# The norms' factors computed on columns with tokens on the partitions, in a two-block transformer kernel

## The chip, the cores and the metric

The kernel runs on one core of one Trainium2 chip. The metric is the device time of one execution in microseconds (us), the median of three. Five engines work on their own queues of instructions, each in order: TensorE (PE in the profile; its weight loads are PEld), VectorE (DVE), ScalarE (ACT), GpSimd (POOL) and SyncE (SP), which issues the weights' transfers. They meet at semaphores.

## The reference

Everything is fp32, one batch, T = 256 tokens, width D = 2048. Two blocks follow each other; the norms are what matters here.

```python
def rms_norm(x, g):
    y = x * lax.rsqrt(jnp.mean(x * x, axis=-1, keepdims=True) + 1e-6)
    return y * g

def first_block(x, mem, ...):            # two layers
    mem_n = rms_norm(mem, mem_norm_g)    # 256 memory tokens, read by 4 heads per layer
    for l in range(2):
        h = rms_norm(x, norm_g[l])
        z = h @ w_in[l]                  # q, k, v and gates of three kinds of attention
        ...                              # neighbourhood, dilated and memory attention
        x = x + y @ w_out[l]
    return rms_norm(x, final_g)

def layer_norm(x, g, b, eps=1e-5):
    mu = x.mean(-1, keepdims=True)
    var = jnp.square(x - mu).mean(-1, keepdims=True)
    return (x - mu) * lax.rsqrt(var + eps) * g + b

def second_block(x, positions, ...):     # ALPHA = sqrt(2)
    for layer in range(2):
        x = layer_norm(ALPHA * x + mixers[layer](x), *ln1[layer])
        x = layer_norm(ALPHA * x + conv_ffn(x, *ffns[layer]), *ln2[layer])
    return x

def mla_rwkv_mixer(x, ...):              # mixers[0]
    c_q, c_kv, k_pe = split_cols(mla_p, (448, 128, 64))
    q = rms_norm_2(c_q, q_norm) @ w_uq   # a norm over 448 latent ranks
    kv = rms_norm_2(c_kv, kv_norm) @ w_ukv   # and one over 128
    ...
```

Each norm needs, for every token, one factor (the reciprocal root of the mean square or the variance), and a layer norm also the shift, minus the mean times the factor.

## The kernel before

The activations lie with features on the 128 partitions and tokens along the free axis: x is 16 tiles of 128x256. The weights (579.8 MB read in all) stream through four raw buffers of 128x1024. ACT rounds each to a high half (`hi`, L2688), DVE subtracts to get the low half (`lo`, L3026), and TensorE does three matmuls for each 128x128 block, high by high, high by low and low by high (`col`, L2185 to L2187, "main matmuls" below). One buffer of weights is 24 of them.

The order of work is written by a Python planner. `do(name, ...)` appends a step to a plan, and each engine's program replays the plan in that order, so every engine has a fixed queue. Side work (norms, attention heads, memory) is written as generators; `pump()` advances each of them by one `yield` after every buffer of weights. A `yield` between two steps therefore sets 24 main matmuls between them on TensorE. `load` keeps the high halves four buffers ahead (AHEAD = 4), and five pairs of halves exist. PSUM is eight banks, handed out by `bank()` and given back with the event that frees them.

Factors are made at ten places. Seven are a `Norm` (class at L717): two for the first block's layers (kind "pre"), the first block's last one, four layer norms. Two generators call `rms_job` (L711): `mem_norm` in `first()` for the memory, and `rank_norms` for q_norm (four tiles) and kv_norm (one tile), so three jobs.

In all of them the squares are summed over the partitions by a matmul with a 128x128 matrix of ones stationary and 256 tokens streamed (`norm_sums`, L2265 and L2266; `rms_sq`, L2247 for each tile). The result is a 128x256 block in a bank in which every partition holds the same sums. The arithmetic is then done on the whole 128x256 block: DVE makes the variance (L3080 to L3087, L3089, L3034), ACT the root (L2705, L2701), DVE the reciprocal (L3094, L3036) and for a layer norm the product (L3097). The result R is a row of factors on all partitions, ready for products with tokens on the free axis: `rms_scale` L3041, `norm_ln` L3140 and L3142, `norm_rms` L3148, `lead_scale` L3134, `lead_fix`, `q_scale` L3184, `gate_evict` L3199 and L3201.

The first block's v has tokens on the partitions, so its two norms also need the factor as a column: `norm_cols` (L2272) takes R through TensorE, two matmuls of one streamed column, into a second bank, and DVE copies it out (L3101) for `v_scale` on ACT.

The memory's attention touches the change too: scores (L2291 to L2293), row maxima on DVE (L3235), exponentials on ACT (L2782, with a table load), normalising on DVE (L3244 to L3247), turning by TensorE (L2302), copies by ACT and DVE (L2773, L3178) and the product with v (L2313 to L2315).

## Time and profile before

| what | us |
|---|---|
| median of 3 runs | 3438.81 (3436.49 to 3444.06) |
| profiled execution | 3437.72 |
| its span in the trace | 3435.9 |
| TensorE busy (weight loads) | 3349.4, 97% (3267.1, 95%) |
| DVE busy | 2304.6, 67% |
| ACT busy | 1629.0, 47% |
| GpSimd busy | 60.2, 2% |
| mean granted TensorE clock | 0.989 of full speed |

The span runs from the first to the last instruction; the profiled execution's own time is 1.8 us longer. Busy times are of single engines and overlap. In the timeline rows, the first column is the start in us from the start of the span, the second the length; in brackets stands the idle time of the engine before the instruction and what ended it. A matmul's length includes its passage through the array, so the distance between two starts (0.11 to 0.12 us for a main matmul), not the length (0.28), is what it costs. An fp32 matmul can be two rows (x2).

### The profile page before, as it was taken

What the parts mean: (1) busy time and instruction counts of PE and PEld (TensorE: products, weight loads), DVE (VectorE), ACT (ScalarE), POOL (GpSimd) and SP (SyncE); (2) the same over time, 40 slices, a digit from 0 to 9 for tenths busy, and PEclk for the clock granted to TensorE, in tenths of its full rate; (3) what the DMA queues carried; (4) which work ended last, traced back from release to release, by engine and by line L of the source; (5) the groups of instructions that cost most, each with busy time, mean ns of one, the idle gap of its engine ahead of it and who ended that gap; (6) DMA issues with size and microseconds to landing.
All of it is one profiled execution on the core that took longest, in us unless ns stands there. A gap on an engine that the chain in (4) does not pass through costs nothing.

```text
span 3435.9 us, 67619 instructions
## 1 busy us (share of the span) xinstructions
PE 3349.4 (97%) x29402; PEld 3267.1 (95%) x29402; DVE 2304.6 (67%) x3765; ACT 1629.0 (47%) x2389; POOL 60.2 (2%) x78
## 2 busy tenths in 40 slices
PE   8999999999999899999999999999999999999997
PEld 8999999999999889999999999998999999999997
DVE  6677656667776787796666555686656966666455
ACT  6444544444555434464444444563443644444443
POOL 0000000000000000000000000001000000000000
PEclk9999999999999999999999999999998999999998
DMA  7555555555554223356555665543434565555563
GB/s 247 176 172 181 180 178 180 188 181 181 175 192 141 89 87 105 111 184 198 192 193 193 196 194 189 177 154 103 157 129 138 170 206 193 193 193 191 188 202 126
DMA packets 162489, 586.29 MB, mean 171 GB/s; under 512 B 18128, under 2 KB 18128, under 8 KB 161936
## 3 DMA queue, kind: packets, MB, share of 16 engines
q1 hardware_dynamic: 160560, 574.01, 51.5%
q0 software_dynamic: 1632, 7.96, 0.7%
q8 instruction: 230, 3.77, 0.5%
q14 instruction: 67, 0.55, 0.1%
HBM read 579.80 MB, written 2.10 MB: 169 GB/s over the span
## 4 chain that ended last, share of the span: by engine, by line
PE 53%; DVE 8%; ACT 1%; issue 0%; POOL 0%; ACTq 0%; DVEq 0%; POOLq 0%
PE bank L2185 16%; PE bank L2187 16%; PE bank L2186 16%; DVE pairs L3026 2%; PE bank L2422 1%; PE bank L2435 1%; DVE xs L3142 1%; DVE xs L3140 1%; PE bank L2200 0%; PE bank L2201 0%; PE bank L2202 0%; DVE xr L3030 0%; DVE right L3513 0%; DVE xr L3110 0%; ACT pairs L2688 0%
## 5 line engine op out<-in xcount | busy, mean ns | idle before, releaser
L2185 PE MATMUL bank<-xr,pairs 128*128 128x256 f32 (+1 forms) x5888 | 1656.9, 281 | 31.0 <-DVE pairs L3026 25.6
L2186 PE MATMUL bank<-xr,pairs 128*128 128x256 f32 (+1 forms) x5888 | 1640.0, 279 | 0.0
L2187 PE MATMUL bank<-xr,pairs 128*128 128x256 f32 (+1 forms) x5888 | 1639.6, 278 | 0.0
L2688 ACT ACTIVATE pairs<-raw 128x1024 fp32r<-128x1024 f32 x1106 | 1144.2, 1042 | 945.4 <-PE bank L2187 716.8
L3026 DVE TENSOR_TENSOR pairs<-raw,pairs 128x1024 fp32r<-128x1024 f32 x1106 | 1311.2, 1202 | 298.2 <-ACT pairs L2688 292.7
L2185 PEld LDWEIGHTS bank<-xr,pairs 128*128 128x128 f32 x5888 | 1114.4, 189 | 43.5 <-DVE pairs L3026 28.3
L2186 PEld LDWEIGHTS bank<-xr,pairs 128*128 128x128 f32 x5888 | 1112.6, 189 | 0.9
L2187 PEld LDWEIGHTS bank<-xr,pairs 128*128 128x128 f32 x5888 | 1113.4, 189 | 0.0
L2185 PE MATMUL bank<-parts,pairs 128*128 128x256 f32 x1792 | 496.2, 277 | 0.4 <-DVE parts L3030 0.4
L2187 PE MATMUL bank<-parts,pairs 128*128 128x256 f32 x1792 | 495.3, 276 | 0.0
L2186 PE MATMUL bank<-parts,pairs 128*128 128x256 f32 x1792 | 495.3, 276 | 0.0
L2185 PEld LDWEIGHTS bank<-parts,pairs 128*128 128x128 f32 x1792 | 336.6, 188 | 0.7 <-DVE parts L3030 0.6
L2186 PEld LDWEIGHTS bank<-parts,pairs 128*128 128x128 f32 x1792 | 336.5, 188 | 0.1
L2187 PEld LDWEIGHTS bank<-parts,pairs 128*128 128x128 f32 x1792 | 336.4, 188 | 0.0
L3487 DVE TENSOR_SCALAR arena<-bank,vec 128x256 f32<-128x256 f32 x88 | 47.8, 543 | 204.2 <-PE bank L2187 204.1
L3154 DVE SCALAR_TENSOR_TENSOR xs<-xs,bank 128x512 f32<-128x512 f32 x64 | 43.5, 686 | 158.9 <-PE bank L2187 158.9
L2713 ACT ACTIVATE nbuf<-xs 128x512 f32<-128x512 f32 x56 | 35.4, 632 | 121.7 <-DVE xs L3056 89.6
L2237 PE MATMUL bank<-pairs,xr 128*128 128x512 f32 x192 | 76.9, 401 | 0.0
L2185 PE MATMUL bank<-yr,pairs 128*128 128x256 f32 x256 | 72.6, 284 | 3.4 <-DVE yr L3030 3.4
L2239 PE MATMUL bank<-pairs,xr 128*128 128x512 f32 x192 | 75.7, 394 | 0.0
L2238 PE MATMUL bank<-pairs,xr 128*128 128x512 f32 x192 | 75.2, 392 | 0.0
L2186 PE MATMUL bank<-yr,pairs 128*128 128x256 f32 x256 | 72.1, 282 | 0.0
(621 smaller groups left out, 3231.6 us busy)
## 6 DMA issues: line engine op xcount, KB each, us to landing
raw<-in_w_in SPq DMA_DIRECT2D x176, 512.0 KB, 4.9
raw<-in_gate SPq DMA_DIRECT2D x176, 512.0 KB, 5.7
raw<-in_val SPq DMA_DIRECT2D x176, 512.0 KB, 4.2
raw<-in_down SPq DMA_DIRECT2D x160, 512.0 KB, 4.4
raw<-in_l_w_in SPq DMA_DIRECT2D x144, 512.0 KB, 4.0
raw<-in_w_out SPq DMA_DIRECT2D x64, 512.0 KB, 4.5
raw<-in_l_w_out SPq DMA_DIRECT2D x64, 512.0 KB, 3.8
raw<-in_v_in SPq DMA_DIRECT2D x48, 512.0 KB, 3.9
```

The costliest lines, as they stand in the source:

```text
L2185: mm(o, wh[:, q, :], rh[:, k, :], start=begin and q == 0, stop=False)
L2186: mm(o, wh[:, q, :], rl[:, k, :], start=False, stop=False)
L2187: last = mm(o, wl[:, q, :], rh[:, k, :], start=False, stop=end and q == c - 1)
L2237: mm(o, lh[:, k, ms], wh[:, q, :], start=k == 0, stop=False)
L2238: mm(o, ll[:, k, ms], wh[:, q, :], start=False, stop=False)
L2239: last = mm(o, lh[:, k, ms], wl[:, q, :], start=False, stop=k == KT - 1)
L2422: last = mm(p4[b, g, :], j.XT[b, g, 64:128], j.X[b, g, :], start=True, stop=True)
L2688: e.activation(pair_of(n)[0], v3(raw_of(n), widths[n] // slices[n]), ACT.Copy).then_inc(*hi_made(n))
L2713: e.activation(N.sq, x[:, t:t + 2, :], ACT.Square).then_inc(*act("norm_sq", N.id, t))
L3026: e.tensor_tensor(lo_, v3(raw_of(n), widths[n] // slices[n]), hi_.bitcast(F32), SUB).then_inc(*lo_made(n))
L3154: e.scalar_tensor_tensor(out=x[:, t:t + 2, :], in0=x[:, t:t + 2, :], scalar=alpha, in1=v3(bk.view, 2), op0=MUL, op1=ADD).then_inc(*vec("x_ ...
L3487: e.tensor_scalar(b, p2[:, 0, :], VC(f"cw2_{l}", t), VC(f"cb_{l}", t), MUL, ADD).then_inc(*vec("conv2", j.id))
```

## The change

The sums get the squares as the stationary operand and one column of ones as the streamed one. The result is one column for each 128 tokens with the tokens on the partitions, so two columns for all. Variance, root, reciprocal and product run on 128x2 blocks in the factor buffer (`nfac`, or two columns for each rms job; `nbuf` is 12 columns wider). The pause (`yield`) between variance and reciprocal goes, one comes after the reciprocal, and behind it stand `norm_rows` or `rms_rows`: TensorE transposes of the column, broadcast along the free axis, give the same row block in a bank as before, and ACT copies it to where R was. Users of the row wait for ACT's copy ("nR", "R" of ACT); `v_scale` takes the columns as they are, and `norm_cols` with its bank is gone. The sums' bank is kept until the copy.

```diff
-    nbuf = sb("nbuf", 6 * T + 12)
+    nbuf = sb("nbuf", 6 * T + 24)
...
+    nfac = nbuf[:, 6 * T + 12:6 * T + 18]
...
@@ class Norm, rows
             yield from self.sums()
-            yield
-            self.bk2 = yield from bank()
-            do("norm_cols", self)
-            banks.put(self.bk2, (vec, "cols", self.id))
@@ class Norm, sums
             do("norm_sums", self)
             yield
             do("norm_var", self)
-            banks.put(self.bk, (vec, "nvar", self.id))
-            yield
             do("norm_R", self)
+            yield
+            do("norm_rows", self)
+            banks.put(self.bk, (act, "nR", self.id))
@@ mem_norm
             do("rms_R", r)
-            banks.put(r.bk, (vec, "var", r.id))
+            yield
+            do("rms_rows", r)
+            banks.put(r.bk, (act, "R", r.id))
@@ rank_norms
             for r in rs:
                 do("rms_R", r)
-                banks.put(r.bk, (vec, "var", r.id))
+            yield
+            for r in rs:
+                do("rms_rows", r)
+                banks.put(r.bk, (act, "R", r.id))
@@ TensorE's program
-            mm(r.bk.view[:, 0:T], ones[rows], r.sq[t].view[rows], start=t == 0, stop=t == r.n - 1).then_inc(*pe("rms", r.id, t))
+            for m in range(2):
+                last = mm(r.bk.view[:, m:m + 1], r.sq[t].view[rows, m * 128:(m + 1) * 128], ones[rows, 0:1],
+                          start=t == 0 and m == 0, stop=t == r.n - 1)
+            last.then_inc(*pe("rms", r.id, t))
+
+        def rms_rows(r):
+            w.wait_ge(*vec["rcol", r.id])
+            for m in range(2):
+                last = e.transpose(r.bk.view[:, T + m * 128:T + (m + 1) * 128], r.f[:, m:m + 1].broadcast_to([128, 128]), ident)
+            last.then_inc(*pe("rrows", r.id))
...
-            if N.kind == "ln":
-                mm(ps[:, 0:T], ones, N.a1, start=True, stop=True)
-            mm(ps[:, T:2 * T], ones, N.a2, start=True, stop=True).then_inc(*pe("norm_sums", N.id))
-
-        def norm_cols(N):
-            w.on(N.bk2.after)
-            w.wait_ge(*vec["nR", N.id])
-            for m in range(2):
-                last = mm(N.bk2.view[:, m:m + 1], N.a2[:, m * 128:(m + 1) * 128], ident[:, 0:1], start=True, stop=True)
-            last.then_inc(*pe("cols", N.id))
+            for i, src in enumerate((N.a1, N.a2)):
+                if i or N.kind == "ln":
+                    for m in range(2):
+                        c = 2 * i + m
+                        last = mm(ps[:, c:c + 1], src[:, m * 128:(m + 1) * 128], ones[:, 0:1], start=True, stop=True)
+            last.then_inc(*pe("norm_sums", N.id))
+
+        def norm_rows(N):
+            w.wait_ge(*vec["ncol", N.id])
+            for c in range(0 if N.kind == "ln" else 2, 4):
+                last = e.transpose(N.bk.view[:, c * 128:(c + 1) * 128], N.f[:, c:c + 1].broadcast_to([128, 128]), ident)
+            last.then_inc(*pe("nrows", N.id))
@@ ACT's program
         def rms_R(r):
             w.wait_ge(*vec["var", r.id])
-            e.activation(r.R, r.R, ACT.Sqrt).then_inc(*act("std", r.id))
+            e.activation(r.f, r.f, ACT.Sqrt).then_inc(*act("std", r.id))
+
+        def rms_rows(r):
+            w.wait_ge(*pe["rrows", r.id])
+            e.activation(r.R, r.bk.view[:, T:2 * T], ACT.Copy).then_inc(*act("R", r.id))
...
+        def norm_rows(N):
+            w.wait_ge(*pe["nrows", N.id])
+            if N.kind == "ln":
+                e.activation(nbuf[:, 4 * T:6 * T], N.bk.view, ACT.Copy).then_inc(*act("nR", N.id))
+            else:
+                e.activation(N.a2, N.bk.view[:, T:2 * T], ACT.Copy).then_inc(*act("nR", N.id))
...
-            w.wait_ge(*vec["nR", j.norm.id])
+            w.wait_ge(*act["nR", j.norm.id])
@@ DVE's program
-            e.tensor_scalar(r.R, r.bk.view[:, 0:T], 1.0 / r.width, 1e-6, MUL, ADD).then_inc(*vec("var", r.id))
+            e.tensor_scalar(r.f, r.bk.view[:, 0:2], 1.0 / r.width, 1e-6, MUL, ADD).then_inc(*vec("var", r.id))
             w.wait_ge(*act["std", r.id])
-            e.reciprocal(r.R, r.R).then_inc(*vec("R", r.id))
+            e.reciprocal(r.f, r.f).then_inc(*vec("rcol", r.id))
...
-            ps, R, nm = N.bk.view, N.a2, N.a1
+            ps, nm, R, m2 = N.bk.view, N.f[:, 0:2], N.f[:, 2:4], N.f[:, 4:6]
...
-                e.tensor_scalar(nm, ps[:, 0:T], -1.0 / D, None, MUL).then_inc(*vec("mean", N.id))
+                e.tensor_scalar(nm, ps[:, 0:2], -1.0 / D, None, MUL).then_inc(*vec("mean", N.id))
...
-            R, nm = N.a2, N.a1
+            nm, R = N.f[:, 0:2], N.f[:, 2:4]
             w.wait_ge(*act["nstd", N.id])
-            e.reciprocal(R, R).then_inc(*vec("nR" if N.kind != "ln" else "nR0", N.id))
+            e.reciprocal(R, R).then_inc(*vec("ncol" if N.kind != "ln" else "nR0", N.id))
```

How the queues change is shown at two places. The lines are numbered by each kernel's own text: before's L2688, L2692, L2760, L2773 and L2782 are L2707, L2711, L2790, L2803 and L2812 now, L3026, L3140 and L3142 are L3056, L3165 and L3167.

ACT's queue at the memory's norm, before: the root of the memory's factors (L2701), then a high half, then the table and the exponentials of the memory attention.

```order
L2701 ACT_TABLE_LOAD
L2701 ACTIVATE arena<-arena 128x256
L2688 ACTIVATE pairs<-raw 128x8x128
L2782 ACT_TABLE_LOAD
L2782 ACTIVATE arena<-arena 128x256 x4
L2688 ACTIVATE pairs<-raw 128x8x128
L2692 ACTIVATE parts<-hs 128x256
L2760 ACTIVATE arena<-bank 128x256
L2773 ACTIVATE heads<-bank 128x512 x2
L2692 ACTIVATE parts<-hs 128x256
```

The same place now:

```order
L2720 ACT_TABLE_LOAD
L2720 ACTIVATE nbuf<-nbuf 128x2
L2707 ACTIVATE pairs<-raw 128x8x128
L2724 ACTIVATE arena<-bank 128x256
L2812 ACT_TABLE_LOAD
L2812 ACTIVATE arena<-arena 128x256 x4
L2707 ACTIVATE pairs<-raw 128x8x128
L2790 ACTIVATE arena<-bank 128x256
L2711 ACTIVATE parts<-hs 128x256
L2803 ACTIVATE heads<-bank 128x512 x2
```

The copy of the rows, L2724, now stands between the high half and the exponentials' table load. On TensorE its two transposes (L2263) stand 48 main matmuls behind the scores and 24 ahead of the turning of the probabilities, which before stood 72 behind the scores.

DVE's queue at layer 0's first layer norm, before: the last sums of squares, two low halves, the variance, a low half, reciprocal and product, a low half, and the first pair of tiles scaled (L3140).

```order
L3074 TENSOR_TENSOR nbuf<-nbuf 128x256
L3026 TENSOR_TENSOR pairs<-raw,pairs 128x8x128 x2
L3080 TENSOR_SCALAR nbuf<-bank 128x256
L3082 TENSOR_TENSOR nbuf<-nbuf 128x256
L3084 SCALAR_TENSOR_TENSOR nbuf<-bank,nbuf 128x256
L3087 TENSOR_SCALAR nbuf<-nbuf 128x256
L3026 TENSOR_TENSOR pairs<-raw,pairs 128x8x128
L3094 RECIPROCAL nbuf<-nbuf 128x256
L3097 TENSOR_TENSOR nbuf<-nbuf 128x256
L3026 TENSOR_TENSOR pairs<-raw,pairs 128x8x128
L3140 TENSOR_TENSOR xs<-xs,nbuf 128x512
```

The same place now:

```order
L3104 TENSOR_TENSOR nbuf<-nbuf 128x256
L3056 TENSOR_TENSOR pairs<-raw,pairs 128x8x128 x2
L3110 TENSOR_SCALAR nbuf<-bank 128x2
L3112 TENSOR_TENSOR nbuf<-nbuf 128x2
L3114 SCALAR_TENSOR_TENSOR nbuf<-bank,nbuf 128x2
L3116 TENSOR_SCALAR nbuf<-nbuf 128x2
L3123 RECIPROCAL nbuf<-nbuf 128x2
L3126 TENSOR_TENSOR nbuf<-nbuf 128x2
L3056 TENSOR_TENSOR pairs<-raw,pairs 128x8x128 x2
L3165 TENSOR_TENSOR xs<-xs,nbuf 128x512
```

The reciprocal stands directly behind the variance, with both low halves behind it. On TensorE the sums stay where they were, and the four transposes (L2291) stand 48 main matmuls behind them, as they do at every `Norm` but the last, where they follow at once.

## Rows read from the trace of the kernel before

**Rows 1.** the page: count, busy us, mean ns, idle us before, releaser.

```profile
L2185 PE MATMUL bank<-xr,pairs 128*128 128x256 f32 (+1 forms) x5888 | 1656.9, 281 | 31.0 <-DVE pairs L3026 25.6
```

**Rows 2.** timeline of TensorE around the memory's norm: start, us, line, idle before.

```profile
86.64 0.28 PE L2293 MATMUL bank<-heads 128*128 128x256 f32 x1
...
94.53 0.28 PE L2185 MATMUL bank<-xr,pairs 128*128 128x256 f32 x1
...
95.24 1.04 PE L2302 MATMUL bank<-con,arena 128*128 128x128 f32 x8
...
98.26 0.36 PE L2313 MATMUL bank<-heads 128*128 128x256 f32 x1 [1.97 <-DVE heads L3178]
```

**Rows 3.** the same stretch on ACT.

```profile
86.68 1.28 ACT L2782 ACT_TABLE_LOAD   x1
...
89.87 0.19 ACT L2782 ACTIVATION_READ_ACCUMULATOR arena<-arena 128x1 f32 x1
...
96.22 1.08 ACT L2773 ACTIVATE heads<-bank 128x512 fp32r<-128x512 f32 x2
```

**Rows 4.** the same stretch on DVE.

```profile
85.35 1.75 DVE L3036 RECIPROCAL arena<-arena 128x256 f32<-128x256 f32 x1 [1.96 <-ACT arena L2701]
...
94.76 0.16 DVE L3244 RECIPROCAL arena<-arena 128x2 f32<-128x2 f32 x1
...
97.43 1.28 DVE L3178 TENSOR_TENSOR heads<-bank,heads 128x512 fp32r<-128x512 f32 x2
```

**Rows 5.** busy time by stretch, PEclk the granted clock.

```profile
96.00:100.00 4.00, 2.03 (x15) 1.82 (x14) 3.11 (x7) 2.67 (x5) 1.09 (x1) 0.90 0.30 114
...
100.00:104.00 4.00, 4.00 (x26) 4.00 (x26) 3.54 (x6) 1.56 (x4) 0.00 (x0) 0.67 0.21 46
```

**Rows 6.** groups of instructions, each shape apart: busy us, mean ns.

```profile
L3244 DVE RECIPROCAL arena<-arena 128x2 f32<-128x2 f32 x40 | 6.3, 157 | 2.6 <-ACT arena L2782 2.3
...
L2760 ACT ACTIVATE arena<-bank 128x256 f32<-128x256 f32 x32 | 12.3, 384 | 122.4 <-DVE bank L3199 122.4
...
L2804 ACT ACTIVATE right<-bank 128x512 f32<-128x512 f32 x10 | 6.0, 598 | 11.4 <-PE bank L2375 10.6 <-PE bank L2346 0.5
```

**Rows 7.** the latent ranks' norms, on DVE, then TensorE.

```profile
1039.29 0.38 DVE L3041 SCALAR_TENSOR_TENSOR arena<-arena,vec 128x256 f32<-128x256 f32 x1
...
1047.88 0.38 PE L2185 MATMUL bank<-xr,pairs 128*128 128x256 f32 x1 [1.80 <-DVE pairs L3026]
...
1053.03 0.58 PE L2385 MATMUL bank<-con,right 128*128 128x2 f32 x4 [0.54 <-ACT right L2832]
```

**Rows 8.** layer 0's first layer norm: sums, 5.7 us of L2185, first user.

```profile
1476.08 0.38 PE L2266 MATMUL bank<-nbuf,con 128*128 128x256 f32 x1
...
1476.50:1482.20 5.70, 4.53 (x16) 2.91 (x16) 1.00 0.71 220
...
1483.19 0.68 DVE L3140 TENSOR_TENSOR xs<-xs,nbuf 128x512 f32<-128x512 f32 x1
```

**Rows 9.** the same two ends at the second and third layer norm.

```profile
2200.73 0.38 PE L2266 MATMUL bank<-nbuf,con 128*128 128x256 f32 x1
...
2207.34 0.68 DVE L3140 TENSOR_TENSOR xs<-xs,nbuf 128x512 f32<-128x512 f32 x1
...
2699.54 0.38 PE L2266 MATMUL bank<-nbuf,con 128*128 128x256 f32 x1
...
2706.68 0.68 DVE L3140 TENSOR_TENSOR xs<-xs,nbuf 128x512 f32<-128x512 f32 x1
```

**Rows 10.** the last norm, on DVE.

```profile
3416.66 0.42 DVE L3080 TENSOR_SCALAR nbuf<-bank 128x256 f32<-128x256 f32 x1 [1.28 <-PE bank L2266]
...
3421.05 0.69 DVE L3140 TENSOR_TENSOR xs<-xs,nbuf 128x512 f32<-128x512 f32 x1
```

**Rows 11.** two stretches of main matmuls: length, TensorE busy (count), granted clock.

```profile
422.80:507.90 85.10, 85.10 (x725) 85.07 (x723) 48.95 (x63) 39.20 (x49) 0.00 (x0) 1.00 0.57 179
...
898.70:980.10 81.40, 80.99 (x715) 80.80 (x713) 52.43 (x71) 40.90 (x54) 1.09 (x2) 1.00 0.60 199
```

54 lines of the change are left out of this document (27 added, 27 removed).

## The prediction

> **What bounds the kernel now.** I read the page's busy times first. TensorE is the bound: its main matmuls wait for little, and nearly all of that for the low halves of weights from DVE: the first of the three lines has 5888 matmuls and 31.0 us of idle time before them, 25.6 of it for L3026 [rows 1]. So DVE's saved time counts only where TensorE waits for DVE, and ACT's only where DVE waits for ACT. A norm's factors matter by the time at which their first user can start, and by what stands behind them in a queue. Next I read the timeline of the three engines around each of the ten places where factors are made, with the order of before and after beside it. They fall into five: the memory's norm, the latent ranks' norms, three layer norms under streamed weights, the last norm, and the rest.
>
> **The change part by part.** All chains run now: sums on TensorE, factor arithmetic on DVE and ACT (two columns), then, about one or two pumps later, transposes on TensorE, and a copy from the bank by ACT. The long DVE operations go, but the user waits for the second TensorE visit, which stands at a fixed place among the main matmuls. Below I ask only when that visit can come.
>
> *The memory's norm.* The last score matmul starts at 86.64 [rows 2]. In the changed order 48 main matmuls follow, then the two transposes. Six main matmuls took 0.71 us (94.53 to 95.24), 0.118 each [rows 2], so the transposes start at 86.76 + 5.66 = 92.4. Eight transposes took 1.04 us, 0.13 each [rows 2]; two end at 92.7. ACT copies 128x256 from a bank in 0.38 us [rows 6], with a hand-off on either side: 93.1. Now the queue: before, ACT began the exponentials' table at 86.68 and ended the last exponential at 90.06 [rows 3]. Now the copy stands in ACT's queue directly ahead of that table, so the table is loaded from 93.1 to 94.4 (1.28 us) and the four exponentials, 2.1 us from 87.98 to 90.06, end at 96.5, 6.4 us later than before. DVE's normalising of the second pair of rows began at 94.76 [rows 4], well after its exponentials, so 4.7 us of the 6.4 are cover; what is left over is 96.5 - 94.76 = 1.7 us. Behind the exponentials ACT has one high half (1.05), then the gate's tanh (which waits for DVE's L3199), a 0.4 us rounding and the copies of the turned probabilities, which began at 96.22 [rows 3]. I get 97.5 after the high half, DVE's row work and L3199 done by 97.8, tanh to 98.2, rounding to 98.6: 2.4 us later. These copies, with DVE's L3178 at 97.43 [rows 4], release the matmul that began at 98.26 after 1.97 us of idle TensorE [rows 2]. TensorE has nothing else in between, so the idle time grows to 4.4: **+2.4 us**. The reciprocal of 1.75 us on DVE that goes [rows 4] gives nothing, as its user, the scaling, isn't on that path. Behind this stop the granted clock falls: 0.90 in the 4 us around it and 0.67 in the next 4 [rows 5], that is 0.4 + 1.3 = 1.7 us of TensorE work lost already. A stop twice as long may add between nothing and as much again; I take the middle, **+0.8**. The ends for this place: +0 (the cover is larger than I think) and +2.4 + 1.7 + 0.4 for queue effects = +4.5.
>
> *The latent ranks' norms.* The scaling began at 1039.29 on DVE, right behind the second reciprocal [rows 7]. The two 1.75 us reciprocals go, but the transposes stand 48 main matmuls behind the last squares, and then ACT copies twice; I get the rows at about 1041.0, 1.7 later. What was late before is another thing too: TensorE stood 1.80 us at 1047.88 for a low half that DVE made behind the scaling [rows 7]. Two low halves now come ahead of the scaling in time, since DVE is free sooner, and this stop should go or shrink. But the user at 1053.03 waits for the chain that starts with the scaling [rows 7], and there the idle time comes back: the chain keeps its end within some tenths, as ACT's and DVE's pauses between its links (0.5 each) are filled differently. **0**, with ends -1.8 (stop gone and nothing back) and +1.7 (the whole lateness).
>
> *The three layer norms whose factors are used under weights* (layer 0's first and second, layer 1's first). The sums' second matmul started at 1476.08 and takes 0.44, to 1476.5. 16 L2185, so 48 main matmuls, took 5.70 us [rows 8]: 1482.2. Four transposes at 0.13: 1482.7. The 512-wide copy 0.60 [rows 6] and two hand-offs: 1483.4, against the first user at 1483.19 [rows 8]: +0.2. At the second the same working from 2200.73 gives 2208.1 against 2207.34, +0.8; at the third from 2699.54 gives 2706.9 against 2706.68, +0.2 [rows 9]. DVE saves in each norm the difference of six long operations and six short ones of 0.16 us [rows 6], near 3 us, but all of them lie ahead of a wait for the rows, so DVE just idles. After these points DVE is the engine that is late until TensorE stands for it, so I count the lateness in full, **+1.2**. The transposes' own 0.5 us fall into those stops. Ends: 0 and 1.2 + 3 x 0.5 = 2.7.
>
> *The last norm.* Here nothing covers anything. Before: DVE 3416.66 to the first scaling at 3421.05, 4.39 us [rows 10]. Now: four operations of 0.16 with 0.05 between them 0.8, a short root 0.25 (bounded by 0.42, the wide one's duration), reciprocal and product 0.4, four transposes 0.5 (up to 1.0 if the clock is low there), copy and hand-offs 0.7: 2.7 to 3.2. **-1.3**, ends -1.7 and -0.9.
>
> *The rest.* The two norms ahead of the first block's layers and the one that ends it: two matmuls with one streamed column replace one with 256. I have no row for such a one alone; it lies between a 128-column transpose, 0.13, and the 0.44 of the wide one, and I take 0.22, which makes the sums equal. The column step (two matmuls, DVE's copy, one bank) goes twice, -0.9; six transposes come, +0.8. Memory squares: 16 tiles at the same price. Their rows come when the reciprocal's result did, give or take 0.3. **0**, ends -1 and +1. The factor buffer is 12 columns wider, which moves what lies behind it by some bytes; no duration in the trace hangs on that.
>
> The transposes' price is the place where the notes speak against the change. The trace's eight took 0.13 us each. The Trainium skill (TensorE: Matmul & The Clock Gate, Part 4: PE-mode transpose) gives about 275 ns for one inside a kernel and says that they don't count as busy time for the clock. By that figure the change's 28 transposes would take 4 us more than mine, of which the half in open places would show: the sum would be 2 us higher. The measured 0.13 decides; whether the clock takes them as idle no row here shows.
>
> **Sum**: +2.4 + 0.8 + 0 + 1.2 - 1.3 + 0 = +3.1. The profiled execution took 3437.7 us (span 3435.9 and 1.8 around it), which gives 3440.8. The median of the timed runs, 3438.8, lies 1.1 above the profiled one, so the median of the changed kernel would be 3440.8 to 3441.9; I say **3441.5**.
>
> **Rivals.** *A: the rows are not what comes last (faster).* If the wait that I see at 1482.7 is covered, DVE's saving of 2.7 to 3 us in each of three norms reaches TensorE, which waits mostly for DVE [rows 1]: -8.1. With the ranks' stop gone (-1.8), the end's -1.3 and only +1 at the memory's norm the time is 3437.7 - 10.2 = 3427.5. For it: the waits for L3026. Against it: the 48 matmuls [rows 8], which no faster engine shortens. *B: ACT's copy holds back high halves (slower).* Behind each copy in ACT's queue stand the high halves that were made before at some 3 us earlier; in the three layer norms a late half of 2.7 us means a late low half and a stop of TensorE. It decides if fewer than two finished pairs lie ready when the copy waits. Price 3 x 2.7 = 8.1 instead of the 1.2 counted: 3440.8 + 6.9 = 3447.7. For: three of the long waits for L3026 follow layer norms. Against: none begins within 15 us of the copies. *C: the pitch of the main matmuls flips.* They run at one of two pitches at full clock: 725 in 85.1 us, 0.1174 each, and 715 in 81.4, 0.1138 [rows 11]. I see flips behind groups of small matmuls, and the change edits such groups. One stretch of 720 at the other pitch is 2.6 us, of either sign; two are 5.2. That gives 3436 to 3447. *D: nothing of it reaches the end*, because the memory's stall was already as long as its cover allows and the clock recovers: 3438.
>
> **How the numbers follow.** Forecast 0.38, A 0.12, B 0.14, C 0.20, D 0.16. A measurement of this kernel can tell about 0.2%, 6.9 us, from no change: faster is under 3431.9, slower above 3445.7. Faster: A, and a small part of C, 0.13. Slower: B, a quarter of C and a rest of the forecast, 0.20. Same: 0.67. The unknown costs' ends lie below the sum by 3.2 (memory), 1.8 (ranks), 1.2, 1 and 0.4, and above it by 1.3, 1.7, 1.5, 1 and 0.4; as not all fall on one side at once, the forecast's own range is 3436 to 3446; with C's second stretch and part of A and B it becomes 3433 to 3450.
>
> **What would show it.** ACT idle for some 6 us before its 256-wide copy of the memory's factors, and TensorE idle for over 4 us before the first probability matmul: right. If that stop is still near 2 us, the memory's term is wrong. DVE idle for 3 to 4 us before the first scaling of each layer norm: right; if it is busy there, A. TensorE waits for L3026 within 10 us behind a layer norm's copy: B. The wait at 1047.88 smaller and the one at 1053 larger: the ranks' term. The first scaling of the last norm 3.1 us behind the end of its sums: the last term. The same number of main matmuls in a longer or shorter stretch without any idle time: C.

## The result and the profile after

The changed kernel took 3444.24 us (median of 20 runs, 3439.35 to 3449.95) against 3439.02 us for the kernel before (20 runs, 3434.24 to 3445.67). The ratio is 1.0015, 95% interval 1.0009 to 1.0021: slower by 0.15%, 5.2 us, with 3 to 7 us in the interval. That is inside the 0.2% that the prediction called no change, and inside its range; it said 2.7 us for the medians. For the profiled execution it said 3.1 us; that execution has a span of 3444.0 us, 8.1 above the one before.

The page of the changed kernel, as answer to [rows 1] (L2193 is what L2185 was, L3056 what L3026 was):

```profile
span 3444.0 us, 67794 instructions
...
PE 3352.3 (97%) x29486; PEld 3271.7 (95%) x29486; DVE 2286.1 (66%) x3763; ACT 1630.8 (47%) x2399; POOL 59.9 (2%) x78
...
L2193 PE MATMUL bank<-xr,pairs 128*128 128x256 f32 (+1 forms) x5888 | 1654.1, 281 | 32.1 <-DVE pairs L3056 24.8
```

The waits of the main matmuls on low halves are what they were, 24.8 against 25.6 us. DVE's busy time is 18.5 us lower, and nothing of it shows in the span.

Because every main matmul (23,808 in all) is in both traces in the same order, the start of each can be subtracted from the start of the same one in another trace. This table holds, for stretches of the kernel (named by the times of the kernel before), how much longer the stretch took than in the first trace of the kernel before, in us. It is worked out from the start times of both traces, to about 0.1 us; "end" is from the last main matmul to the end of the span.

| kernel | 12-70 | 70-130 memory | 130-540 | 540-975 | 975-1022 | 1022-1100 ranks | 1150-1240 | 1475-1600 LN | 2195-2330 LN | 2330-2700 | 2700-2760 LN | end |
|---|---|---|---|---|---|---|---|---|---|---|---|---|
| before, second trace | +1.2 | +0.2 | 0.0 | +2.9 | +0.2 | 0.0 | 0.0 | -0.3 | +0.1 | -3.2 | +0.2 | +0.9 |
| changed | +0.8 | +2.5 | -0.8 | +0.5 | +1.8 | +1.1 | +2.8 | +0.6 | +1.0 | -4.1 | +1.1 | -0.4 |
| changed, second trace | +0.4 | +2.1 | -1.6 | +3.4 | +0.7 | +3.0 | +3.1 | +0.2 | +0.9 | -1.6 | +0.3 | -1.0 |

The two traces of one kernel show what a single one can tell: many stretches agree within 0.4 us, but 12 to 70, 540 to 975, 2330 to 2700, the end and, in the changed kernel, 130 to 540, 975 to 1022, the third layer norm's and the ranks' stretch move by 0.6 to 3 us by themselves. What repeats is +2.3 at the memory's norm, +0.2 to +1.1 at each layer norm and 3 us between 1150 and 1240; the end is about 1.2 shorter in the mean (-0.7 against +0.45).

**The memory's norm.** ACT in the changed kernel, as answer to [rows 3]: start, length, in brackets the idle time before.

```profile
94.20 0.38 ACT L2724 ACTIVATE arena<-bank 128x256 f32<-128x256 f32 x1 [5.79 <-PE bank L2263]
94.61 1.28 ACT L2812 ACT_TABLE_LOAD   x1
...
97.79 0.18 ACT L2812 ACTIVATION_READ_ACCUMULATOR arena<-arena 128x1 f32 x1
...
101.64 1.06 ACT L2803 ACTIVATE heads<-bank 128x512 fp32r<-128x512 f32 x2
```

TensorE in the same stretch, as answer to [rows 2] (L2263 the new transposes, L2321 the turning of probabilities, L2332 the product with v):

```profile
88.02 0.28 PE L2312 MATMUL bank<-heads 128*128 128x256 f32 x1
...
93.79 0.38 PE L2263 MATMUL bank<-con,nbuf 128*128 128x128 f32 x2
...
97.90 0.66 PE L2321 MATMUL bank<-con,arena 128*128 128x128 f32 x4 [1.00 <-DVE arena L3272]
99.73 0.66 PE L2321 MATMUL bank<-con,arena 128*128 128x128 f32 x4 [1.17 <-DVE arena L3272]
103.08 0.55 PE L2332 MATMUL bank<-heads 128*128 128x256 f32 x1 [2.70 <-DVE heads L3203]
```

The last score matmul is at 88.02, 1.38 later than before by what lies ahead. From it the transposes are 5.77 us away, the copy comes after 5.79 us of idle ACT, and the last exponential ends at 97.97 instead of 90.06: 7.9 later, 6.5 net of the 1.38. The single stop of 1.97 us has become three, of 1.00, 1.17 and 2.70, together 4.87. The probability product starts 4.82 us later, 3.4 of it the change's. Behind it a part comes back, at the end 0.16 us in every 4 by a faster pitch of the main matmuls; at 130 us 2.5 are left. The stops differ between two traces of one kernel too: the second trace of the kernel before has 2.82 us where the first has 1.97, the second of the changed kernel 1.00, 0.33 and 3.18. In the mean of two traces each that is 4.7 against 2.4 us, 2.3 more.

**The layer norms.** DVE at layer 0's first layer norm, as answer to [rows 8]:

```profile
1487.25 0.15 DVE L3110 TENSOR_SCALAR nbuf<-bank 128x2 f32<-128x2 f32 x1
...
1488.47 0.16 DVE L3126 TENSOR_TENSOR nbuf<-nbuf 128x2 f32<-128x2 f32 x1
...
1493.56 0.69 DVE L3165 TENSOR_TENSOR xs<-xs,nbuf 128x512 f32<-128x512 f32 x1 [2.65 <-ACT nbuf L2733]
```

The six short operations take 1.4 us from 1487.25 to 1488.63 with the root among them; two low halves follow, and then DVE idles 2.65 us for ACT's copy. Net of what lies ahead (10.0 us by then) the first scaling starts 0.37 later than before. The stops of TensorE behind it are as long as they were: the first is 2.13 and 1.81 us in the two traces of the changed kernel, 2.13 and 1.79 in those of the kernel before.

**The last norm.** As answer to [rows 10], DVE:

```profile
3425.93 0.16 DVE L3110 TENSOR_SCALAR nbuf<-bank 128x2 f32<-128x2 f32 x1 [2.02 <-PE bank L2285]
...
3429.15 0.69 DVE L3165 TENSOR_TENSOR xs<-xs,nbuf 128x512 f32<-128x512 f32 x1 [1.84 <-ACT nbuf L2733]
```

From the first operation to the first scaling it is 3.22 us, before 4.39.

**The ranks' norms.** TensorE's waits in the whole span, as answer to the stops of [rows 7]:

```profile
PE bank L2404 <- ACT right L2862: 5.3, 3, 3.9
```

The longest, 3.9 us, is the user that stood 0.54 us before; the stop of 1.80 for a low half is gone. The user itself is not late: it starts at 1057.91, 4.9 us behind the 1053.03 of the kernel before, and TensorE was 5.5 us late already at 1022. Yet the stretch lost 1.1 and 3.0 us, and nothing in the second trace of the kernel before. What lies elsewhere is time at half clock: both traces of the kernel before have 3.41 us of it ahead of the user (from 1048.1 in the first), the changed kernel behind it (from 1058.4), and its second trace 3.41 us more from 1032.5, where it falls back by 1.6.

### The profile page after: what moved, and what is told of

Read it like the earlier page. It is cut to its first block, busy times and chain, and to the rows that moved or that the text cites. A ratio compares the mean times of both kernels' runs of the same rounds, so it can differ in the third digit from the quotient of the medians.

```text
span 3444.0 us, 67794 instructions
## 1 busy us (share of the span) xinstructions
PE 3352.3 (97%) x29486; PEld 3271.7 (95%) x29486; DVE 2286.1 (66%) x3763; ACT 1630.8 (47%) x2399; POOL 59.9 (2%) x78
## 4 chain that ended last, share of the span: by engine, by line
PE 89%; DVE 7%; ACT 2%; issue 1%; DMA 1%; POOL 0%; ACTq 0%; SPq 0%; DVEq 0%; POOLq 0%
PE bank L2193 25%; PE bank L2195 24%; PE bank L2194 24%; DVE pairs L3056 2%; PE bank L2245 2%; PE bank L2247 2%; PE bank L2246 2%; PE bank L2441 1%; PE bank L2454 1%; DVE xs L3167 1%; ACT pairs L2707 1%; DVE xr L3060 1%; DVE xs L3165 1%; DMA raw<-in_w_in 0%; PE bank L2208 0%
## 5 line engine op out<-in xcount | busy, mean ns | idle before, releaser
L2193 PE MATMUL bank<-xr,pairs 128*128 128x256 f32 (+1 forms) x5888 | 1654.1, 281 | 32.1 <-DVE pairs L3056 24.8
L2707 ACT ACTIVATE pairs<-raw 128x1024 fp32r<-128x1024 f32 x1106 | 1144.0, 1042 | 932.9 <-PE bank L2195 726.9
L3056 DVE TENSOR_TENSOR pairs<-raw,pairs 128x1024 fp32r<-128x1024 f32 x1106 | 1310.4, 1202 | 296.0 <-ACT pairs L2707 290.4
L2193 PEld LDWEIGHTS bank<-xr,pairs 128*128 128x128 f32 x5888 | 1111.5, 189 | 43.3 <-DVE pairs L3056 27.2
L2193 PE MATMUL bank<-parts,pairs 128*128 128x256 f32 x1792 | 495.9, 277 | 0.4 <-DVE parts L3060 0.4
L2193 PEld LDWEIGHTS bank<-parts,pairs 128*128 128x128 f32 x1792 | 336.4, 188 | 0.6 <-DVE parts L3060 0.6
L2193 PE MATMUL bank<-yr,pairs 128*128 128x256 f32 x256 | 72.2, 282 | 4.1 <-DVE yr L3060 4.1
```

What stands on the lines that cost most here:

```text
L2193: mm(o, wh[:, q, :], rh[:, k, :], start=begin and q == 0, stop=False)
L2707: e.activation(pair_of(n)[0], v3(raw_of(n), widths[n] // slices[n]), ACT.Copy).then_inc(*hi_made(n))
L3056: e.tensor_tensor(lo_, v3(raw_of(n), widths[n] // slices[n]), hi_.bitcast(F32), SUB).then_inc(*lo_made(n))
```

## The experiments

All medians stand beside runs of the kernel before on the same chip; with 11 or 12 runs they carry an interval of about 0.9 thousandths, 3 us, to each side (ln_rows24, 6 runs, 1.4 thousandths). So the place of an effect is read from the stretches, the medians only confirm large ones. The stretches of all kernels, against the first trace of before:

| kernel | ratio (95% interval) | 70-130 memory | 975-1022 | 1022-1100 ranks | 1150-1240 | 1475-1600 LN | 2195-2330 LN | 2700-2760 LN | end |
|---|---|---|---|---|---|---|---|---|---|
| changed | 1.0015 (1.0009-1.0021) | +2.5, +2.1 | +1.8, +0.7 | +1.1, +3.0 | +2.8, +3.1 | +0.6, +0.2 | +1.0, +0.9 | +1.1, +0.3 | -0.4, -1.0 |
| mem_undone | 1.0010 (1.0000-1.0020) | +0.3 | +1.8 | +2.7 | +2.8 | +0.4 | +0.9 | +0.3 | -1.1 |
| mem_copy_later | 1.0017 (1.0008-1.0026) | -0.2 | +0.7 | +3.0 | +2.9 | +0.9 | +0.9 | +0.1 | -0.5 |
| ranks_undone | 1.0018 (1.0008-1.0027) | +1.9 | +1.8 | +1.8 | +2.8 | +0.2 | +0.9 | +0.6 | -0.5 |
| ln_undone | 1.0015 (1.0006-1.0024) | +2.7 | +1.8 | +2.7 | +3.0 | 0.0 | +0.1 | +0.8 | +0.8 |
| rms_undone | one run | +3.4 | 0.0 | +1.4 | +2.8 | +0.4 | +1.0 | +1.1 | -0.4 |
| rms_rows24 | 0.9998 (0.9989-1.0007) | -0.8 | +1.8 | +0.3 | +1.7 | +0.4 | +0.9 | +0.6 | -0.8 |
| norm_rows_early | 1.0009 (1.0000-1.0018) | +3.7 | +1.8 | +2.0 | +0.4 | -0.2 | +0.2 | -0.7 | -1.3 |
| all_pace | 1.0002 (0.9994-1.0011) | +0.4 | +1.8 | +4.9 | +2.9 | -0.4 | +0.2 | -0.2 | -0.7 |
| all_rows_early | 0.9995 (0.9986-1.0004) | -0.8 | +0.6 | +2.3 | +0.4 | -0.2 | +0.2 | 0.0 | -1.2 |
| ln_rows24 | 1.0048 (1.0035-1.0062) | +2.5 | +0.7 | +3.1 | +3.1 | +1.1 | +3.7 | +2.9 | -1.3 |

Five edits leave the memory's norm as the changed kernel has it (ranks_undone, ln_undone, rms_undone, norm_rows_early, ln_rows24). With the changed kernel's own two traces the memory's stretch is then +1.9 to +3.7. TensorE runs 3.41 us at half clock behind the stop in the four with +1.9 to +2.5, and 6.83 us in the three with +2.7 to +3.7.

### The memory's norm as before

```diff
+            if r.wide:   # the memory's job: PE, ACT, DVE steps of the kernel before
+                mm(r.bk.view[:, 0:T], ones[rows], r.sq[t].view[rows], start=t == 0, stop=t == r.n - 1).then_inc(*pe("rms", r.id, t))
+                return
...
             do("rms_R", r)
-            yield
-            do("rms_rows", r)
-            banks.put(r.bk, (act, "R", r.id))
+            banks.put(r.bk, (vec, "var", r.id))
```

> The changed kernel with the memory's norm alone as it was before (wide sums, wide root and reciprocal, no transposes, no copy). Theory (ACT's copy of the rows holds back the exponentials): ACT's 5.8 us of idle time before the copy and TensorE's longer stop before the first probability matmul go; that stop is near 2.0 us again instead of 2.7 behind two of about 1, the main matmuls behind it start about 2.8 us earlier against the changed kernel, and the median is 2 to 4 us lower. Rival (small matmuls and the pitch of the main ones make the difference, not this wait): the stop shrinks but the median moves by less than 1 us.

Measured: +0.3 instead of +2.5 and +2.1 in the memory's stretch, with one stop of 2.80 us in place of the three (not the 2.0 that was expected, but the 2.82 of the second trace of before); the ratio goes from 1.0015 to 1.0010, which is in the expected direction but not told apart by the interval. So 2 us belong to this place.

### ACT's copy behind the exponentials

The transposes stay where they are; only the step that holds ACT's copy is planned one pump later.

```diff
-            do("rms_rows", r)
-            banks.put(r.bk, (act, "R", r.id))
-            for t in range(KT):
-                yield
-                yield
+            do("rms_turn", r)      # TensorE's two transposes
+            yield
+            do("rms_copy", r)      # ACT's copy
+            banks.put(r.bk, (act, "R", r.id))
+            for t in range(KT):
+                if t:
+                    yield
+                yield
```

> The changed kernel with one instruction moved: ACT's copy of the memory's rows stands behind the four exponentials and the next high half instead of ahead of them; TensorE's and DVE's queues are the same. Theory (the copy in front of the exponentials is the whole cost at the memory's norm): the exponentials end near 91 us again, the stop before the first probability matmul is 2 to 3 us and those before the turning go, main matmuls behind it 2 to 2.8 us earlier than in the changed kernel. Rival (the transposes on TensorE, or DVE's later scaling, are the cost): TensorE reaches 130 us as late as in the changed kernel, within 0.7.

Measured, ACT (L2815 the exponentials, L2727 the copy), then TensorE (L2266 the transposes, L2335 the product with v):

```profile
86.99 1.28 ACT L2815 ACT_TABLE_LOAD   x1
...
90.18 0.18 ACT L2815 ACTIVATION_READ_ACCUMULATOR arena<-arena 128x1 f32 x1
...
93.14 0.38 ACT L2727 ACTIVATE arena<-bank 128x256 f32<-128x256 f32 x1 [1.82 <-PE bank L2266]
...
92.72 0.38 PE L2266 MATMUL bank<-con,nbuf 128*128 128x128 f32 x2
...
99.38 0.55 PE L2335 MATMUL bank<-heads 128*128 128x256 f32 x1 [2.67 <-DVE heads L3206]
```

The table load starts at 86.99, right behind the high half, the last exponential ends at 90.36, and the copy waits where nobody needs ACT. The three stops are one of 2.67 us again. The stretch 70 to 130 takes 0.2 us less than before and 2.3 to 2.7 less than in the changed kernel, with TensorE's and DVE's queues the same. The trace shows the mechanism by itself: neither the transposes nor the later rows cost more here than the 0.2 to 0.4 us by which a stretch scatters; the place of one 0.38 us copy in ACT's queue does. Its median (5.9 us over before, interval 2.7 to 8.9) does not show the gain: the stretch 540 to 975 took 3.4 us more in its trace, as in the second traces of both kernels, and that is the size of the interval that a median of 11 runs has. The proof rests on the stretches of the traces, not on the medians.

### The latent ranks' norms as before

The same edit for the other two jobs.

> The changed kernel with the latent ranks' norms alone as before. Theory: the stop of 3.9 us before the L2404 matmul goes back to 0.5 us and a stop of about 1.8 for a low half comes back 5 us ahead of it; net 0.5 to 1.5 us faster than the changed kernel. Rival (the ranks' norms cost what their later rows say, plus the stretches at half clock behind them at 1167, 1198 and 1283 us): 3 to 5 us faster.

Measured: +1.8 in the ranks' stretch, between the +1.1 and +3.0 of the changed kernel's own two traces; ratio 1.0018. The theory's 0.5 to 1.5 us do not come. The stop for a low half is back (1.71 us, with 0.39 ahead of it), but the user's goes from 3.9 to 2.14 and not to 0.5. The user starts at 1054.65, on time against its surroundings, but the 3.41 us at half clock still lie behind it (from 1055.5), and not ahead as in the kernel before. So no gain or loss of these norms is seen, and the stretch's 1 to 3 us go with the place of the half clock; no run moved that on purpose. The rival's 3 to 5 us are excluded for this stretch, and the 2.8 us between 1150 and 1240 stay.

### The layer norms as before

The same edit for the Norms of kind "ln".

> The changed kernel with the four layer norms as before (wide sums and arithmetic, no transposes); the other norms stay changed. Theory: the three layer norms under weights give back 1.2 us and TensorE's transposes there 0.3 each, and the last norm gets 0.4 us longer: 0.5 to 2 us faster than the changed kernel. Rival (the layer norms hold a large part of the 5 us): 3 us faster or more. Second rival (the layer norms were a gain): slower by 1 us or more.

Measured: 0.0 and +0.1 in the first two stretches where the changed kernel has +0.6, +0.2 and +1.0, +0.9; +0.8 in the third, which scatters. The end is 0.8 over the first trace of before, the second trace of before had 0.9. The ratio, 1.0015, is the changed kernel's. The theory's 0.5 to 2 us are not seen: its 0.4 for the last norm was too little (the end is 1.5 us longer than in the changed kernel's mean), which cancels the 1.3 us of the first two layer norms. None of this is clear of a median's interval of 3 us.

### Rows 24 main matmuls behind the sums, layer norms, pause removed

```diff
             do("norm_R", self)
-            yield
+            if self.kind != "ln":
+                yield
             do("norm_rows", self)
```

> The changed kernel, layer norms only: the pause between reciprocal and transposes removed, so that the transposes stand 24 instead of 48 main matmuls behind the sums. Theory (the rows are what comes last at the three layer norms, and DVE is what TensorE waits for afterwards): the first scaling of each starts 2.6 to 2.8 us earlier, TensorE's following stops for low halves shrink by as much, the median is 5 to 8 us lower than the changed kernel. Rival (those stops come from elsewhere, transfers or ACT): DVE's scaling starts earlier, but the stops stay and the median moves by less than 2 us.

Measured: 11 us slower than the changed kernel by the ratios, the opposite of both. The theory's first half held: DVE waited only 0.97 us for the copy, at 1490.29, and against its surroundings the first scaling starts 2.9 us earlier than in the changed kernel.

```profile
1490.29 0.69 DVE L3166 TENSOR_TENSOR xs<-xs,nbuf 128x512 f32<-128x512 f32 x1 [0.97 <-ACT nbuf L2734]
...
1517.62 0.38 PE L2194 MATMUL bank<-xr,pairs 128*128 128x256 f32 x1 [2.58 <-DVE pairs L3057]
```

But the removed pause lets the generators of side work run one buffer ahead, and the planner deals out other work to the following buffers. At 1517.62 TensorE stands 2.58 us for a low half that DVE made behind other work. In layer 1's mixer 5 us are lost in the stretch 2330 to 2560 against the changed kernel. The same 45 us of the clock hold 676 matmuls there and 582 here; as ln_rows24 is 3 to 7 us later at this point, the two windows do not hold the same work. The changed kernel,

```profile
2355.00:2400.00 45.00, 45.00 (x676) 42.68 (x675) 29.91 (x62) 18.40 (x31) 3.33 (x5) 1.00 0.37 118
```

and ln_rows24:

```profile
2355.00:2400.00 45.00, 44.00 (x582) 39.98 (x581) 26.92 (x55) 15.57 (x27) 3.34 (x5) 0.96 0.33 104
```

The edit had moved two things. That the moved side work is the cause is concluded from this; the next edit moves one thing only.

### The same rows, the pace of the side work kept

```diff
             do("norm_R", self)
-            yield
             do("norm_rows", self)
+            yield
             banks.put(self.bk, (act, "nR", self.id))
```

DVE's queue is now that of the changed kernel (but for one low half near 110 us, which stands one place earlier); only transposes and copy stand earlier, at every Norm.

> The changed kernel with the transposes of every Norm 24 instead of 48 main matmuls behind its sums, while the side work keeps its pace (the pause now stands behind the transposes), so that DVE's queue is the same and only the transposes and ACT's copy move. Theory (rows are what comes last at the three layer norms and DVE's lateness reaches TensorE; the slower ln_rows24 got slower because its side work moved by one buffer): the first scalings start 2.6 us earlier against their surroundings, DVE's idle time of 2.7 to 3.3 us before them goes, the stops for low halves behind them shrink by 1 to 2.6 us each, and the median is 3 to 7 us lower than the changed kernel's. Rival (earlier rows themselves do harm, as in ln_rows24): slower than the changed kernel by 5 us or more. Second rival (the stops are set by ACT's high halves or the transfers): within 1.5 us.

Measured: DVE no longer waits for the copy, but now it waits 1.92 us for a high half, ahead of the low half in front of the scaling. DVE, then ACT:

```profile
1486.60 1.22 DVE L3056 TENSOR_TENSOR pairs<-raw,pairs 128x1024 fp32r<-128x1024 f32 x1
1489.74 1.23 DVE L3056 TENSOR_TENSOR pairs<-raw,pairs 128x1024 fp32r<-128x1024 f32 x1 [1.92 <-ACT pairs L2707]
1490.88 0.69 DVE L3165 TENSOR_TENSOR xs<-xs,nbuf 128x512 f32<-128x512 f32 x1
...
1488.16 0.60 ACT L2733 ACTIVATE nbuf<-bank 128x512 f32<-128x512 f32 x1 [1.87 <-PE bank L2291]
1488.66 2.00 ACT L2707 ACTIVATE pairs<-raw 128x1024 fp32r<-128x1024 f32 x2
```

In ACT's queue that high half stands behind the copy, and the copy waits 1.87 us for the transposes: it is the memory's mechanism again, and that of the prediction's rival B. The idle time of DVE does not go, it shrinks from 2.65 to 1.92 us, by 0.7. The first scaling starts 0.8 us earlier against its surroundings, not 2.6.

The stop that was 2.13 us in the changed kernel's first trace (1.81 in its second) is 1.39:

```profile
1520.33 0.39 PE L2193 MATMUL bank<-xr,pairs 128*128 128x256 f32 x1 [2.13 <-DVE pairs L3056]
...
1524.32 0.39 PE L2193 MATMUL bank<-xr,pairs 128*128 128x256 f32 x1 [0.97 <-DVE pairs L3056]
```

```profile
1517.65 0.38 PE L2193 MATMUL bank<-xr,pairs 128*128 128x256 f32 x1 [1.39 <-DVE pairs L3056]
...
1521.65 0.39 PE L2193 MATMUL bank<-xr,pairs 128*128 128x256 f32 x1 [0.99 <-DVE pairs L3056]
```

The three stretches gain 0.6, 0.8 and 1.4 us on the changed kernel (mean of its traces), 2.7 together. The median ratio falls from 1.0015 to 1.0009, 2.1 us, inside the interval. The theory is right in kind and its 3 to 7 us were too many: it took DVE's whole idle time as won, and what TensorE got, 0.7 us of 2.13, is what was left of it once DVE waited for the high half. A copy placed behind that high half was not tried.

### The memory's and the ranks' rows 24 matmuls earlier; all together

rms_rows24 removes the pause ahead of `rms_rows` in both generators; all_pace moves all transposes ahead of their pauses; all_rows_early joins rms_rows24 and norm_rows_early.

> The changed kernel, memory's and latent ranks' norms only: the pause between reciprocal and transposes removed (24 instead of 48 main matmuls). Theory: ACT copies the memory's rows 2.8 us earlier, the exponentials end 2.8 us earlier, and since 4.7 us of delay were covered before, hardly any of the memory's 2.8 us are left; the ranks' user comes 2.5 us earlier too. Together 4 to 5.5 us faster than the changed kernel. Rival (the small instructions themselves and not their place cost the time): under 1.5 us.

> As norm_rows_early, and the memory's and the latent ranks' transposes 24 instead of 48 main matmuls behind the squares too, again with the pace kept. Theory: the two gains add, as they lie at different places: 7 to 12 us below the changed kernel, 2 to 6 below the kernel before. Rival (only the memory's place is worth anything): 4 to 6 us below the changed kernel, level with the kernel before.

> The version that the runs point to: the changed kernel with the memory's and the ranks' rows as in rms_rows24 and the Norms' rows as in norm_rows_early. Theory (effects at separate places add, the memory and ranks' 1.2 us better than the changed kernel's by the matmuls' times, the layer norms' 3.3 us, the last norm's gain stays): 8 to 10 us below the changed kernel, 3 to 5 us below the kernel before, so a ratio of 0.9985 to 0.999. Rival (the places don't add because a gain before 1100 us is lost again at the stop near 1165 us): level with the kernel before within 1.5 us.

Measured for rms_rows24: the memory's stretch is 0.8 below before and 3.1 below the changed kernel, the ranks' 0.3 above before, ratio 0.9998, that is 6 us below the changed kernel. So a copy that comes one buffer earlier removes the change's cost. The 0.8 us beyond it are the clock's: the stop here is 2.81 us, longer than the 1.97 of before, but no half clock comes behind it, in this trace and in that of all_rows_early. Like ln_rows24 this edit also moved side work; all_pace, which kept the pace, has the same earlier copy and +0.4. The 6 us agree with the first expectation, 4 to 5.5, within the interval, and not with the rival's under 1.5. For all_pace: memory +0.4, layer norms as expected, but +4.9 at the ranks, where this edit also placed each job's copy between the two roots on ACT and so set the second job's chain behind the first's (its transposes hold TensorE for 0.76 us at 1040.84, waiting for DVE's reciprocal). The ratio is 1.0002, 4.5 us below the changed kernel where 7 to 12 were expected. For all_rows_early: the places add (memory -0.8, layer norms 0.0, end -1.2), ratio 0.9995 with an interval of 0.9986 to 1.0004. It is 7 us below the changed kernel and level with the kernel before; a gain on the latter, expected as 3 to 5 us, is not shown.

### Where the remaining microseconds are

> The changed kernel with the first block's last norm alone as before. Theory: its two transposes set the slower pitch of the main matmuls behind them, so the 1.8 us that every kernel with the transposes loses between 975 and 1022 us go, within 0.5. Rival (the pitch there comes from what lies earlier): the 1.8 us stay.

Measured, in a single trace: 0.0 in 975 to 1022, where the changed kernel has +1.8 and +0.7. TensorE is never idle there, it only runs main matmuls more slowly. Four traces by stretch, the second column TensorE busy and the count of its matmuls: the kernel before,

```profile
990.00:1020.00 30.00, 30.00 (x267) 30.00 (x266) 23.86 (x46) 15.43 (x21) 0.00 (x0) 1.00 0.52 165
```

the changed kernel,

```profile
990.00:1020.00 30.00, 30.00 (x257) 30.00 (x257) 23.10 (x41) 14.65 (x18) 0.00 (x0) 1.00 0.57 181
```

its second trace,

```profile
990.00:1020.00 30.00, 30.00 (x267) 30.00 (x266) 23.56 (x43) 14.65 (x18) 0.00 (x0) 1.00 0.57 179
```

and rms_undone:

```profile
990.00:1020.00 30.00, 30.00 (x267) 30.00 (x266) 25.10 (x47) 14.00 (x19) 0.00 (x0) 1.00 0.52 172
```

267 matmuls in 30 us are 0.112 each and 257 are 0.117, at full granted clock in all four. These are the two pitches of [rows 11]. But rms_undone took back the norm's sums together with its transposes, and the traces tell them apart. The changed kernel's first trace in the 5 us ahead of the narrow sums (984.67) and in the 5 us behind them, still ahead of the transposes (990.76):

```profile
979.60:984.60 5.00, 5.00 (x47) 5.00 (x46) 3.16 (x5) 2.12 (x2) 0.00 (x0) 1.00 1.00 366
985.60:990.60 5.00, 5.00 (x45) 5.00 (x44) 4.33 (x9) 1.44 (x3) 0.00 (x0) 1.00 0.65 210
```

So the theory's number holds and its cause doesn't: the pitch is slow from the sums on, before any transpose. By the distances of the starts, all eleven traces with this norm changed run at 0.118 between sums and transposes. Seven arrive at 0.113 and stay at 0.118 behind the transposes; four, the changed kernel's second among them (540 to 975: +3.4), arrive at 0.118 and run at 0.113 behind the transposes. With the wide sums the pitch behind is 0.113 in all three traces, also in the second of the kernel before, which arrives at 0.118. So a short group of other matmuls can flip the pitch either way, and what the change costs here depends on which pitch arrives: +1.8 or +0.7. Why a group flips it stays open.

> The changed kernel, unchanged, for a second trace. Theory: the memory's 2.4 us, the layer norms' 2.7, the 1.8 behind the last norm of the first block and the shorter end are there again within 0.7 each, and the stretches at half clock lie elsewhere, so that the 2.8 us between 1150 and 1240 us may be absent. Rival: these 2.8 us are the change's own and are there again.

> The kernel before, unchanged, for a second trace: which of the differences between the two traces (a stretch at half clock at 1167 us and 3 us lost between 1145 and 1245 us; stretches at half clock at 2331 and 2628 us that are longer before) belong to the change and which to one execution. Theory: the 3 us between 1145 and 1245 are not of the change, so this trace shows them too at least in part, and the half-clock time before 3400 us differs from 58 us by several us. Rival: this trace is like the first within 1 us everywhere.

The 2.8 us between 1150 and 1240 are there in both traces of the changed kernel and in seven of the ten edits (rms_rows24 has 1.7, norm_rows_early and all_rows_early 0.4), and in neither trace of before, so on this point the theory was wrong both times and the rivals right: they come with the changed kernel, though they lie 110 us behind the nearest edited instruction. On the rest the theories held: the memory's stretch, the layer norms and the end repeat within 0.8 us (0.7 was allowed), only the 1.8 became 0.7; and the half-clock time before 3400 us, summed over all stretches at half clock, was 58 us in the first trace of before and 34 in the second. The granted clock is the seventh column of numbers:

```profile
1150.00:1240.00 90.00, 81.53 (x1076) 74.27 (x1075) 74.45 (x184) 37.12 (x91) 4.72 (x9) 1.00 0.27 86
```

```profile
1150.00:1240.00 90.00, 82.25 (x1042) 75.19 (x1041) 70.63 (x176) 37.70 (x93) 4.72 (x9) 0.94 0.23 75
```

```profile
1150.00:1240.00 90.00, 81.70 (x1061) 74.63 (x1061) 72.00 (x182) 40.18 (x98) 4.72 (x9) 0.98 0.24 78
```

The three are the kernel before, the changed kernel and norm_rows_early. Before, the clock is full throughout, though TensorE starts nothing for 3.4 us behind 1158.77 (idle time 3.08); changed, at the same stop, 3.45 us behind 1165.17 (idle time 3.17), the clock falls to half, and the mean is 0.94; norm_rows_early is between. The loss of the stretch goes with the time at half clock in it: none in both traces of before (0.0 us lost), 3.4 us in norm_rows_early and all_rows_early (0.4), 6.8 in rms_rows24 (1.7), 10.2 in all others (2.8 to 3.1). No instruction of this stretch was edited. The clock falls at a stop in one kernel and not at an equal one in another, and what decides isn't found; no edit here moved it on purpose. It remains open how the change brings it about.

## Why the prediction was right

The forecast was +3.1 us on the profiled execution, where 8.1 came, and 3441.5 for the median, where 3444.2 came, within 3433 to 3450 and on the side of slower. A range of 17 us holds the kernel before as well, so the range alone proves little. By its own steps:

- *The memory's norm*, +2.4 and +0.8 for the clock. The mechanism was right and read closely: exponentials at 96.5 in the kernel before's time (measured 96.6), ACT's 6 us of idle time (5.79). By its own sign TensorE was to idle over 4 us before the first probability matmul; there it was 2.70, and the 4.87 come only with two stops ahead of the turning, where the prediction had nothing in between. Net 2.1 to 2.5 in the changed kernel: the lateness was undersized (3.4 at the product), part of it comes back, and the +0.8 for the clock did not come in its two traces (3.41 us at half clock, as before); in three of the five other traces with this norm it did, at 6.83 us and +2.7 to +3.7. mem_copy_later shows that the copy's place in ACT's queue is all of the cost.
- *The ranks' norms*, 0: the stop of 1.80 went and the idle time came back at the user, as written. The stretch lost 1.1 and 3.0 us all the same; by the traces that goes with the half clock behind the user, which the step did not have; the ends given, -1.8 and +1.7, hold one of the two. ranks_undone keeps +1.8.
- *The three layer norms*, +1.2: the first scalings came 0.4, 0.9 and 0.2 late, the same in every trace with these rows, where 0.2, 0.8 and 0.2 were forecast; the stretches lost 0.4, 0.9 and some 0.7 us. ln_undone removes the first two. Slightly low. The sign was 3 to 4 us of idle DVE; it is 2.65.
- *The last norm*, -1.3: 4.39 us became 3.22, and the end's stretch is 1.2 shorter in the mean of two traces each.
- *The rest*, 0. Between 130 and 540 us the changed kernel gains 0.8 to 1.6; behind the first block's last norm 0.7 to 1.8 are lost by the pitch, rival C's mechanism, which was in the range and not in the sum; and the 2.8 us at half clock near 1165 were in no term.

In the means of two traces each the memory has 2.2, the ranks 2.0, the layer norms 2.0, the last norm -1.2, 130 to 540 -1.2, the pitch 1.2 and the half clock near 1165 2.9: 7.9 of the 8.3 us by which the spans differ. The medians of 20 runs say 5.2, with 3 to 7, so these traces overstate it. The forecast had the direction and the largest named term by their mechanisms. That its median came within 2.7 us (3441.5 against 3444.2) is in part luck: two things that it counted as 0, -1.2 and +1.2, cancel, and for two that don't, the half clock at the ranks and near 1165, it had no term. Rival A (rows hidden, DVE's saving reaches TensorE) is refuted: DVE idles 2.65 us in the layer norm. It was right on what the saving is worth once the rows come earlier, but at a third of its price (0.6 to 1.4 us a norm instead of 2.7). Rival B (late high halves behind ACT's copy) cost nothing in the changed kernel: a high half does stand behind the copy of 1492.93, but DVE waits for the same copy, and the first stop for L3056 behind it ends at 1520.33, at the same main matmul as before. It is what remains once the rows come earlier, as the 1.92 us in norm_rows_early show.

The transposes' price, 0.13 us, can be read now (L2291, first at layer 0's first layer norm, then at the last norm):

```profile
1492.29 0.60 PE L2291 MATMUL bank<-con,nbuf 128*128 128x128 f32 x4
...
3424.06 1.84 PE L2285 MATMUL bank<-con,nbuf 128*128 128x1 f32 x8 [3.31 <-DVE nbuf L3104]
3427.37 1.11 PE L2291 MATMUL bank<-con,nbuf 128*128 128x128 f32 x4 [1.48 <-DVE nbuf L3126]
```

Four take 0.60 us from first start to last end, at most 0.15 each, and 1.11 at half clock. The measured price holds. The Trainium skill (TensorE: Matmul & The Clock Gate, Part 4: PE-mode transpose) gives about 275 ns for one of 128x128 in bf16 in a kernel's context. By that, four would be 1.1 us, an estimate; this case's, in fp32, come to that only at half clock.

## What to carry to other kernels

Price a cheaper computation by the arrival of its result at the first user, not by the time it saves: here 18.5 us less work for VectorE bought 1.2 us, at the one place without cover, and the extra hop through TensorE came at a fixed place in a full queue. When a step adds an instruction to an in-order queue, look at what stands directly behind it: a copy of 0.38 us that waits for another engine held up four exponentials for 6 us. When it is moved, ask what it will then stand in front of: one buffer earlier at the layer norms it held up a high half instead, and 2.65 us of idle time became 1.92. And move such a step without changing the pace of the planner, or the experiment measures the planner.

## What was not expected of the hardware

Main matmuls of one shape run at 0.112 to 0.114 or at 0.117 to 0.119 us each at full granted clock, for hundreds in a row; the state changed at short groups of other matmuls and can differ between two executions of the same program, which is worth up to 2.9 us here (540 to 975, two traces of the kernel before). At a stop of TensorE (3.17 us idle) the clock fell to half in the changed kernel, and at the same stop (3.08 and 3.16 us) it did not in either trace of the kernel before. Streaming one column instead of 256 did not make the sums cheaper: the last norm's eight passes at half clock took 1.84 us, about twice the 0.95 of the same eight in layer 0's first norm at full clock:

```profile
1485.65 0.95 PE L2285 MATMUL bank<-con,nbuf 128*128 128x1 f32 x8
```

That is 0.24 for each of the four matmuls; two of them replace one that took 0.44.
